# Sorted experts: token rows gathered by lists instead of scattered, and expert weights fetched in pairs

## The reference, cut to what matters

```python
scores = sigmoid(t @ w_router)                       # 512 x 16
... choose a group of 4 experts, then 2 experts in it
combine = sum(one_hot(e_idx, 16) * w_sel[..., None], 1)
h = silu(einsum('td,edf->tef', t, w_gate)) * einsum('td,edf->tef', t, w_up)
y = einsum('tef,efd->td', h * combine[..., None], w_down)
```

## Time and profile before

| | |
|---|---|
| median of 3 runs | 4072.62 us |
| profiled execution | 4070.53 us |
| span in it, first to last instruction | 4068.8 us |
| TensorE busy (matmul) | 3582.0 us, 88% |
| VectorE busy | 2836.6 us, 70% |
| ScalarE busy | 846.0 us, 21% |
| GpSimd busy | 896.9 us, 22% |
| `moe`, first vector instruction to last result tile stored | 2748.4 to some 3018 us |

### The profile page before, as it was taken

One profiled execution on the slowest core, in us unless ns is written; L12 is line 12 of the kernel. 1 busy time (PEld: TensorE's weight loads), 2 busy tenths in 40 slices (PEclk: granted clock), 3 DMA queues, 4 the chain that ended last, 5 costly groups with the idle time before them and its releaser, 6 DMA issues. The chain is left out here.

```text
span 4068.8 us, 43607 instructions
## 1 busy us (share of the span) xinstructions
PE 3582.0 (88%) x15846; PEld 2435.1 (60%) x15846; DVE 2836.6 (70%) x5091; ACT 846.0 (21%) x1666; POOL 896.9 (22%) x856
## 2 busy tenths in 40 slices
PE   8999998778778777777999998986988999999998
PEld 6778775223223222222667776865766787877876
DVE  7553678778878877865754466766877558757775
ACT  2111022111111111110121135415852312411000
POOL 2010004444434444443000021204540000100000
PEclk9999999999999999999999998997999999999999
DMA  7322228999999999998334432129962233223221
GB/s 290 137 93 94 96 104 323 420 423 423 423 423 423 423 422 419 410 419 368 113 120 146 146 109 88 51 96 381 416 260 83 79 94 99 83 94 101 96 88 70
DMA packets 206417, 910.08 MB, mean 224 GB/s; under 512 B 20958, under 2 KB 25966, under 8 KB 126738
## 3 DMA queue, kind: packets, MB, share of 16 engines
q0 software_dynamic: 93040, 665.54, 40.0%
q1 hardware_dynamic: 108272, 233.47, 17.1%
q10 hardware_dynamic: 4900, 8.42, 0.6%
HBM read 878.45 MB, written 40.97 MB: 226 GB/s over the span
## 5 line engine op out<-in xcount | busy, mean ns | idle before, releaser
L176 PE MATMUL psum<-ring_high,h_features 128*128 128x512 f32 x1128 | 459.9, 408 | 31.3 <-PEq L48 14.5
L130 DVE CAST ring_high<-ring_raw 128x2048 fp32r<-128x2048 f32 (+2 forms) x163 | 187.9, 1153 | 417.3 <-PE psum L178 340.4
L178 PE MATMUL psum<-ring_high,h_features 128*128 128x512 f32 x1128 | 446.6, 396 | 0.0
L177 PE MATMUL psum<-ring_low,h_features 128*128 128x512 f32 x1128 | 446.2, 396 | 0.0
L1769 PE MATMUL psum<-slots_ring,evacuation_tmp 128*128 128x512 f32 x672 | 333.3, 619 | 91.4 <-DVE evacuation_tmp L1863 91.4
L176 PE MATMUL psum<-h_features,ring_high 128*128 128x512 f32 (+3 forms) x888 | 349.5, 394 | 11.2 <-DVE ring_low L132 4.5
L132 DVE TENSOR_TENSOR ring_low<-ring_raw,ring_high 128x2048 fp32r<-128x2048 f32 (+2 forms) x163 | 349.5, 2144 | 12.6 <-issue 0.4
L177 PE MATMUL psum<-h_features,ring_high 128*128 128x512 f32 (+3 forms) x888 | 346.7, 390 | 0.0
L178 PE MATMUL psum<-h_features,ring_low 128*128 128x512 f32 (+3 forms) x888 | 346.7, 390 | 0.0
L1985 ACT ACTIVATE weight<-score 128x1 f32<-128x1 f32 x512 | 103.6, 203 | 1123.5 <-DVE score L1870 1123.3
L1769 PE MATMUL psum<-slots_features,evacuation_tmp 128*128 128x512 f32 x504 | 251.9, 624 | 63.7 <-DVE evacuation_tmp L1863 63.5
(11 more groups left out here) (679 smaller groups left out, 7020.2 us busy)
## 6 DMA issues: line engine op xcount, KB each, us to landing
ring_raw<-in_w_in SPq DMA_DIRECT2D x94, 1024.0 KB, 5.3
ring_raw<-in_w_up_pairs SPq DMA_DIRECT2D x20, 1024.0 KB, 5.0
ada_ring<-in_w_ada POOLq DMA_DIRECT2D x16, 1024.0 KB, 5.6
ring_raw<-in_w_out SPq DMA_DIRECT2D x12, 1024.0 KB, 5.1
moe_entries<-in_const_zero_rows POOLq DMA_DIRECT2D x23, 512.0 KB, 4.8
row_room<-moe_entries SPq DMA_DIRECT2D x23, 512.0 KB, 11.1
moe_results<-rows_out SPq DMA_DIRECT2D x23, 512.0 KB, 7.6
ring_raw<-in_w_down SPq DMA_DIRECT2D x10, 1024.0 KB, 4.9
```

Source lines behind the costliest of these rows:

```text
L130: nc.vector.tensor_copy(high, whole)
L176: nc.tensor.matmul(out, a[0], b[0], start=start, stop=False)
L177: nc.tensor.matmul(out, a[0], b[1], start=False, stop=False)
L178: return nc.tensor.matmul(out, a[1], b[0], start=False, stop=stop)
```

## The change

Five edits go together.

1. The scratch tensor of sorted rows, its zeroing and the scatter are gone. SyncE instead stores the 512 token rows as they are into `moe_tokens`, in `place_experts`.
2. A list of tokens for each tile row is made on chip. VectorE turns `rows_of` into two sets of one-hot matrices, the tile and the row within the tile, weights one set with the token's number plus one, and TensorE multiplies them (8 products of float32, 23 columns) into a table, row by tile. A zero there is padding and becomes an index past the end.
3. GpSimd gathers each tile's rows from `moe_tokens` by that table; an index past the end is skipped by the bounds check. There are two places for rows instead of four, cleared once in `place_experts`.
4. The gate and up halves of a tile are fetched together as one transfer of 2 MB (`pair`), down alone as 1 MB (`single`); each kind has two places.
5. The four vectors are loaded late in the loop instead of before it.

GpSimd's new order is written out in the diff: pair, rows, single.

```diff
 # second block, first branch (pool_part)
-        for s in range(ROW_TILES):
-            pool.wait_ge(on.updated, s + 1)
-            ...
-            pool.dma_start(core.moe_entries[s * P:(s + 1) * P, :], d["const_zero_rows"]).then_inc(core.entries_cleared, 16)
+        pool.wait_ge(on.updated, 2 * LEVELS - 1)
 ...
 # place_experts, SyncE and GpSimd
+            for t in range(NT):
+                sp.dma_start(core.moe_tokens[t * P:(t + 1) * P, :], core.x[:, t, :]).then_inc(core.tokens_stored, 16)
 ...
+            pool.wait_ge(core.products, QUARTERS * (first + 1))
+            nc.gpsimd.memset(row_room, 0.0).then_inc(cleared, 1)
 ...
-RAW_PIECES, CUT_PIECES, ROW_PLACES = 5, 4, 4
+RAW_PIECES, CUT_PIECES, ROW_PLACES, RAW_PLACES = 5, 4, 2, 2
+NO_TOKEN = 4096.0
 ...
 # moe, GpSimd
-                for t in range(NT):
-                    for which in range(2):
-                        nc.gpsimd.indirect_dma_start(out=entries, out_offset=..., in_=core.x[:, t, :], in_offset=None).then_inc(sorted_rows, 16)
-                pool.wait_ge(pieced, 1)
-                for n, (s, piece) in enumerate(taken):
-                    if n >= RAW_PIECES:
-                        pool.wait_ge(cut_high, n - RAW_PIECES + 1)
-                        pool.wait_ge(cut_low, n - RAW_PIECES + 1)
-                    nc.gpsimd.indirect_dma_start(out=raw[:, n % RAW_PIECES, :], ...).then_inc(piece_in[n % RAW_PIECES], 16)
+                def pair(s):
+                    if s >= RAW_PLACES:
+                        pool.wait_ge(cut_high, turn[s - RAW_PLACES, 1] + 1)
+                        pool.wait_ge(cut_low, turn[s - RAW_PLACES, 1] + 1)
+                    nc.gpsimd.indirect_dma_start(out=pair_place(s), out_offset=None, in_=d["moe_pairs_2"], ...).then_inc(pair_in[s % RAW_PLACES], 16)
+
+                def single(s):
+                    if s >= RAW_PLACES:
+                        pool.wait_ge(cut_high, turn[s - RAW_PLACES, 2] + 1)
+                        pool.wait_ge(cut_low, turn[s - RAW_PLACES, 2] + 1)
+                    nc.gpsimd.indirect_dma_start(out=single_place(s), out_offset=None, in_=d["moe_singles_2"], ...).then_inc(single_in[s % RAW_PLACES], 16)
+
+                def enter(s):
+                    if s >= ROW_PLACES:
+                        pool.wait_ge(row_turned, s - ROW_PLACES + 1)
+                    nc.gpsimd.indirect_dma_start(out=rows_in[:, s % ROW_PLACES, :], out_offset=None, in_=core.moe_tokens,
+                                                 in_offset=bass.IndirectOffsetOnAxis(ap=tokens_of[:, s:s + 1], axis=0),
+                                                 bounds_check=SEQ - 1, oob_is_err=False).then_inc(row_in[s % ROW_PLACES], 16)
+
+                pool.wait_ge(core.tokens_stored, 16 * NT)
+                pool.wait_ge(pieced, 1)
+                pair(0)
+                pool.wait_ge(read, 1)
+                enter(0)
+                enter(1)
+                pair(1)
+                for s in range(2):
+                    single(s)
+                for s in range(2, ROW_TILES):
+                    pair(s)
+                    enter(s)
+                    if s >= 3:
+                        single(s - 1)
+                single(ROW_TILES - 1)
 # moe, SyncE
-                def enter(s):
-                    if s >= ROW_PLACES:
-                        sp.wait_ge(row_turned, s - ROW_PLACES + 1)
-                    sp.dma_start(rows_in[:, s % ROW_PLACES, :], tile(entries, s)).then_inc(row_in[s % ROW_PLACES], 16)
 ...
 # moe, TensorE, ahead of turn_rows(0)
+                pe.wait_ge(spotted, 1)
+                for j in range(2 * NT):
+                    mm = nc.tensor.matmul(core.ps[:, 7, 0:ROW_TILES], on_row[:, j, :], in_tile[:, j, :], start=j == 0, stop=j == 2 * NT - 1)
+                mm.then_inc(listed, 1)
 # moe, VectorE, ahead of the first cut
+                def spot_rows():
+                    all_rows = rows_of[:].rearrange("p t w -> p (t w)")
+                    nc.vector.tensor_single_scalar(spot[:, 0:2 * NT], all_rows, 7, ALU.logical_shift_right)
+                    nc.vector.tensor_single_scalar(spot[:, 2 * NT:4 * NT], all_rows, P - 1, ALU.bitwise_and)
+                    ...
+                    nc.vector.tensor_tensor(in_tile, ..., ALU.is_equal)          # 128 x 184
+                    nc.vector.tensor_tensor(on_row, ..., ALU.is_equal)           # 128 x 1024
+                    nc.vector.tensor_tensor(in_tile, in_tile, token_codes..., ALU.mult)
+                    dve.drain().then_inc(spotted, 1)
+
+                def list_tokens():
+                    dve.wait_ge(listed, 1)
+                    codes = core.ps[:, 7, 0:ROW_TILES]
+                    nc.vector.tensor_scalar(absent[:], codes, 0.5, NO_TOKEN, ALU.is_lt, ALU.mult)
+                    dve.drain()
+                    nc.vector.scalar_tensor_tensor(tokens_of[:], codes, -1.0, absent[:], ALU.add, ALU.add)
+                    dve.drain().then_inc(read, 1)
+                spot_rows()
                 own_tiles()
+                list_tokens()
                 share_out()
```

More of the change, by code:

```diff
@@ L3126, in place_experts @@
             score_row, score, bias, lower_first, chosen, order, placed, sel, pair_sums, best, beats, ties, group_beats, group_ties, rank, g_rank, total, before, resets, kinds, number, whole, tiles, earlier, part, mine, row_f), \
-            stage(nc, "place", "loaded", "squashed", "turned", "ready", "cut", "reset", "chose", "counted") as (
-                block, loaded, squashed, turned, ready, cut, reset, chose, counted):
+            stage(nc, "place", "loaded", "squashed", "turned", "ready", "cut", "reset", "chose", "counted", "cleared") as (
+                block, loaded, squashed, turned, ready, cut, reset, chose, counted, cleared):
         @block.sync
@@ L3283, in moe @@
                      hidden_low=([P, 2, 2, P], F32R), rows_out=[P, 2, D]) as (raw, last_cut, hidden, silu_g, hidden_high, hidden_low, rows_out), \
-                stage(nc, "moe", "sorted", "pieced", "row_turned", "row_high", "row_low", "cut_high", "cut_low", "used_piece", "squashed", "gated",
-                      "hidden_turned", "hid_high", "hid_low", "left", "evacuated", "scaled", "weighted", "merged", "cast", "vectors_loaded", "var_ready", "root_ready", "normed", "transposed", "copied", "lowered", *[f"piece{b}" for b in range(RAW_PIECES)],
+                stage(nc, "moe", "spotted", "listed", "read", "pieced", "row_turned", "row_high", "row_low", "cut_high", "cut_low", "used_piece", "squashed", "gated",
+                      "hidden_turned", "hid_high", "hid_low", "left", "evacuated", "scaled", "weighted", "merged", "cast", "vectors_loaded", "var_ready", "root_ready", "normed", "transposed", "copied", "lowered", *[f"pair{b}" for b in range(RAW_PLACES)], *[f"single{b}" for b in range(RAW_PLACES)],
@@ L3290, in moe @@
[L3290 removed]
+            pair_in, single_in, row_in = more[0:2], more[2:4], more[4:4 + ROW_PLACES]
+            stored, back = more[4 + ROW_PLACES:4 + ROW_PLACES + 2], more[4 + ROW_PLACES + 2:]
+            pair_place = lambda s: raw[:, 2 * (s % RAW_PLACES):2 * (s % RAW_PLACES) + 2, :].rearrange("p a n -> p (a n)")
+            single_place = lambda s: (raw[:, 2 * RAW_PLACES, :], last_single)[s % RAW_PLACES]
@@ L3348, in _ @@
                 load_ahead(core, sp, 2 * values + 2)
[L3349 to L3358, removed]
+                vectors = [(core.row_a[:], d["ln2_g_2"][0]), (core.row_b[:], d["ln2_b_2"][0]), (in_gain, d["in_ln_g_3"]), (in_shift, d["in_ln_b_3"])]
+                sp.wait_ge(read, 1)
+                for s in range(1, ROW_TILES):
+                    leave(s - 1)
+                    if ROW_TILES - 2 * len(vectors) <= s < ROW_TILES - len(vectors):
+                        buf, vec = vectors[s - ROW_TILES + 2 * len(vectors)]
+                        sp.dma_start(buf, vec.partition_broadcast(P)).then_inc(vectors_loaded, 16)
                 leave(ROW_TILES - 1)
@@ L3525, in cut_rest @@
                         dve.wait_ge(used_piece, n - CUT_PIECES + 1)
-                    nc.vector.tensor_tensor(cut(1, n), raw[:, n % RAW_PIECES, :], cut(0, n).bitcast(F32), ALU.subtract).then_inc(cut_low, 1)
+                    nc.vector.tensor_tensor(cut(1, n), raw_piece(*taken[n]), cut(0, n).bitcast(F32), ALU.subtract).then_inc(cut_low, 1)
                 def rest_of_rows(s):
```

79 lines of the change are left out of this document (50 added, 29 removed).

## The result

The changed kernel takes 4118.65 us (median of 4 runs, 4114.26 to 4122.9); the kernel before 4072.11 (4 runs). The ratio is 1.0113, with an interval of 1.0096 to 1.0131: 46.5 us slower, where +21 was forecast and 4111 was the upper end of the range. The sign and the mechanism were right, the size was not. The profiled execution took 4122.9 us, its span is 4121.2.

A forecast was written before the change was run, and what follows sets the result against it. The prediction took DMA engines to pace the kernel before at 10.0 us a tile. Row waits made 10 X - 209.6 = +23.4, less padding +21: 4091.5 profiled, 4093 us forecast median; range 4060 to 4111.

The forecast's parts named there:

- The queue's order: Expert loop: rows queue behind their waiting pair on GpSimd, so TensorE has a 3.0 us gap each two tiles.
- t: Expert loop: the start of tile i's first product, from which the prediction counts its times.
- The stage's own start: Start of the expert stage: without scatters, their landing and the load, the first product comes 10.8 us earlier.
- The rival with the rows in time: Expert loop: rows arrive in time and TensorE sets the pace; X 18.8, 4050 us, chance 0.15.
- the one with a small wait: Expert loop: pair issued before the subtraction, TensorE keeps its clock; X 19.9 to 21.4, 4060 to 4076 us, chance 0.24.
- That padding is not skipped: Rival, row gathers: 0.52 MB of rows move per tile, 0.35 more on X, 3 us later; no chance given.
- a larger transfer: Rival, weight fetches: larger transfers stream faster, each 0.5 us off the pair's landing taking 5 us off; no chance given.
- X: Expert loop: the time for two tiles, forecast at 23.3 us; from 21.0 the start's gain is used up.
- Issue: Pair's issue on GpSimd: mean 1.83 us taken, ends 0.94 with VectorE idle and 2.94 inside a subtraction.
- Landing: Pair's 2 MB transfer in the loop: lands 7.0 us after its issue, 4.5 for a 1 MB gather plus streaming at 422 GB/s.
- Clock: TensorE behind the gap: 3 us mostly at 1.2 GHz instead of 2.4 adds 1.5 us per two tiles.
- The zeroing: Removed zeroing of sorted rows: counted at nothing, since GpSimd only waits between its 23 issues and no engine waits for them.

The follow-up runs named there:

- the kernel with the rows ahead: The changed kernel with GpSimd gathering the rows of tile s+1 right behind pair s, one pair earlier: 4052.29 us, ratio 0.9957 to the kernel before.
- the pairs split: The changed kernel with each 2 MB pair fetched as two 1 MB gathers, the first sent once its half is free: 4117.35 us, ratio 1.0112.
- VectorE is held: The changed kernel with VectorE's third-piece subtraction waiting until the pair three tiles on is issued, marked by a one-column GpSimd fill: 4110.83 us, ratio 1.0098.
- The filler: The changed kernel with 18 unused products of 128 columns before the waiting row transposes of every even tile: 4109.55 us, ratio 1.0097.
- the pair of kernels with the rows ahead: Rows gathered one tile earlier than in the changed kernel, without and with the 23 zeroing transfers put back: 4052.29 us and 4063.72 us.

## Why the prediction missed

**Held.** The queue's order, shown by the kernel with the rows ahead. The pair's issue starts at t + 8.28 (predicted 8.3). TensorE waits in every second tile. The stage's own start gives 9.4 us, where 10.8 was predicted.

The rival with the rows in time fell, and so did the one with a small wait. That padding is not skipped fell too: in the last tiles, which hold padding alone, the rows land 0.2 us behind the pair. Nor did a larger transfer gain anything over two of half its size: with the pairs split the time is 4117.35 us. Of the signs named for the forecast two stand, the DMA share of 0.76 (under 0.9) and no wait of ScalarE for weights. One does not: the wait was to be 2 to 4 us and is 5.4, the 3.0 of the prediction with the errors of issue, landing and rows below.

**The step that failed: the size of X, the time of two tiles**, 23.3 predicted. Between turn_hidden of tiles 0 and 20 twenty tiles took 3040.8 - 2775.1 = 265.7 us, so X is 26.6. Its terms, as means of ten cycles of the timeline (even tiles 4 to 22), which add up to 26.6:

| term, us | predicted | measured |
|---|---|---|
| t to the pair's issue | 8.3 | 8.28 |
| its issue | 1.83 | 2.91 |
| issue's end to the pair's landing | 7.0 | 8.57 |
| rows behind the pair | 0.9 | 0.69 |
| wake-up, transposes, down, turn_hidden, to the next first product | 3.8 + 1.5 | 6.12 |

- *Issue, +1.1.* The mean of the earlier trace rows mixed blocked and free issues. In the changed loop the order is fixed, and nearly every pair's issue meets a subtraction: the median is 2.96, one of the two ends named. Its view in the trace:

```profile
L3335 POOL DMA_INDIRECT raw<-in_moe_pairs,pieces_of x23: 939/2959/2988, 2743.2 to 3022.2; - x23
```

  By the Trainium skill, "SBUF — State Buffer", section "Who interferes with whom", tensor_tensor did not stall a DMA in the probe told there, while a vector instruction with two SBUF inputs contends with a GpSimd instruction that reads SBUF. This trace goes with the second: the gather's issue takes 2.96 us beside such a subtraction, and 0.94 us when VectorE is held. But not all of it can be won back: freed, it gave 8 us by the medians, not 20.
- *Landing, +1.6.* 7.0 was made of a lone 1 MB gather and 422 GB/s, the rate of a loop whose engines always had a next transfer. The packets part it. In the lone gather the first packet started 0.70 us behind the issue's end, and its 1.05 MB landed 3.81 us later. In the ten cycles the pair's first packet starts 1.57 us behind the issue's end in the mean (1.3 in eight of them), 0.9 more, and its 2.1 MB land 7.0 us later, where 3.81 and 2.5 had been taken, 0.7 more. Both begin below the loop's rate, as the first two microseconds show, of the pair in the cycle above and then of the lone gather:

```profile
2866.00:2867.00 1.00, 1.00 (x6) 0.84 (x5) 1.00 (x1) 0.98 (x1) 0.70 (x1) 1.00 1.15 229
2867.00:2868.00 1.00, 1.00 (x6) 0.84 (x5) 1.00 (x2) 0.94 (x1) 1.00 (x1) 1.00 0.68 279
```

```profile
646.00:647.00 1.00, 1.00 (x8) 0.87 (x7) 1.00 (x2) 0.15 (x1) 0.00 (x0) 1.00 0.89 156
647.00:648.00 1.00, 1.00 (x9) 0.92 (x8) 0.86 (x4) 0.90 (x2) 0.00 (x0) 1.00 0.83 336
```

  So a slow beginning alone is not the difference, nor is the results' write. With VectorE held, the first packet comes 0.70 us behind the issue's end again in seven of ten cycles, so the later first packet goes with the blocked issue. But the pair then lands 8.3 us behind its first packet in the mean instead of 7.0, which eats half of what the free issue gains. Why the landing behind the first packet takes 0.7 us more than was taken (the lone gather's packets are of 8 KB, the pair's of 16) stays open.
- *Clock, +0.8.* The gap, 5.94 us in the cycle above, is longer than the 2.66 of the earlier trace rows, and the granted clock behind it is 0.50 (the lower level, 1.2 GHz) until 2879 and 1.00 from 2880 on, just before turn_hidden. The filler's 2.3 us is the whole term, where 1.5 was taken.

Ten such cycles are +33 us, and the 2 to 3 us off for padding tiles did not come (their rows land 0.2 behind the pair, but the pairs there take 8.9 to 9.5).

**The zeroing, counted at nothing.** Its price is 11.4 us by the pair of kernels with the rows ahead. The view read for it, who waits for the zeroing, could not show it: it is no wait on a semaphore. The prediction had no price to fall back on; its 5 us are for the stored tokens and for the late vectors, and no run tried those two. Left out of a forecast that came out too low, this gain made the miss smaller; that is luck.

**The sum again**, on the profiled executions: tile 1 starts 7 us sooner than predicted (10 by the shift ahead of the stage, less 3 inside it; some 6 of the 10 go with the zeroing, and the rest is this execution, whose placing ends earliest of the eleven without it), the loop takes 33 more, no padding is saved (2.5), and from the last turn_hidden to the end it takes 1063.5 us instead of 1059.7 (3.8; the last gathers lie there, no run was made for it): 4091.5 - 7 + 33 + 2.5 + 3.8 = 4124, measured 4122.9.

Two of the prediction's figures do not fit its own working: the sum of all the long ends is 4109, inside the range that is said to leave it out, and the chance of slower, 0.63, is above the 0.61 of the only rival that is slower. And the range gave the landing no spread at all, the term that missed by most.

The rows ahead make the change worth it: 4052.3 us beat both kernels, by 0.43% and 1.6%.

## What to carry to other kernels

When a load moves from a queue of its own into an ordered one, write down what stands in front of it there, and whether its consumer comes earlier than the consumers of what it is queued behind; a reordering of three lines was worth 66 us here. Where an average covers two kinds of events, ask which kind the new order makes permanent, and take a transfer's price from rows where the queue is as empty or as full, and the issue as free or as blocked, as it will be. Transfers that nobody waits for can still cost time: take them out and look at where an engine idles for "issue".

## What was not expected of the hardware

- A drain on GpSimd behind an indirect gather ended with the gather's landing (next issue after 9.68 us), so it cannot mark an issue; a small fill can, 0.11 us.
- 18 products that nothing uses, in front of each wait, did not make the loop slower (4109.55 us): the granted clock of the loop was 0.97 with them, 0.89 without.
- From 2780 to 2980 us the DMA engines were 96% busy at 381 GB/s in the kernel with the rows ahead, and 101% at 413 GB/s in the kernel before: 8% fewer bytes, only 5% less of the engines' time. Why was not tried.
